# Attention products of the second block from split operands, in a two-block layer kernel

## The chip, the core and the metric

The kernel runs on one core of a Trainium2 chip. The metric is the device time of one execution in microseconds. A core has five engines that run their own instruction streams and meet only at semaphores: TensorE (PE in the profile; its weight loads are PEld), VectorE (DVE), ScalarE (ACT), GpSimd (POOL) and SyncE (SP), which here only issues loads.

## What is computed

Two layers in sequence on 512 tokens of width 2048, in fp32. Each is a wide input projection, several mixers, an output projection, a scaled residual and a layer norm. Block 0 mixes with forgetting attention, a short convolution and pooling. Block 1, on which the change works, has attention over selected keys and a state-space mixer:

```
u = einsum('bsd,de->bse', h, w_in)
q, k = rope(q), rope(k)                    # 8 query heads, 2 key/value heads, 128 wide
score = sum over 16 index heads of relu(q_idx . k_idx) * w_idx
_, sel = lax.top_k(score, 128)             # keys each query may attend to
s = (q . k[sel]) * scale ;  p = softmax(s) ;  o_attn = p . v[sel]
o = concat(o_attn * silu(z_attn), ssd(...))
h = layer_norm(alpha * h + o @ w_out)
```

The kernel does not gather. It finds the threshold by 16 rounds of eight maxima and masks all other keys. A block of 128 queries sees only keys up to its own end, so the score products have 128, 256, 384 and 512 columns.

## The kernel before

**Projections.** The weights stream through four slots, one unit of 128 x 1024 each, two units to a tile of 128 output features. For each unit SyncE loads `raw`, ScalarE rounds it to `w_hi` (`round_unit`, L870) and GpSimd computes `w_lo = raw - w_hi` (`low_part`, L409). TensorE multiplies in the one-pass format fp32r: `project` (L480) issues three matmuls of 512 columns for each of 16 row blocks, hi*hi, hi*lo and lo*hi, 48 for a tile. A unit keeps TensorE for about 5.5 us. ScalarE rounds a unit once the one four before it in the same slot has been used, so each unit has some 15 us from use to next use.

**Two kinds of small product.** `mm` on fp32 tiles is a true fp32 product; the trace shows it as two weight loads and two matmul records. `three` (L553) makes one product of three fp32r matmuls from high and low parts. In block 0 the scores and P.V of 256 columns and more already go through `three` (`attn_start1`, L558; `attn_pv1`, L567); the products of 128 columns are fp32 there. In block 1 all are fp32 (`head_scores`, `head_pv`).

**The heads of block 1.** TensorE's order is written out by hand. For head h of 1 to 7: the scores of attention head h-1 (`attn_start2`), the projection of the next q tile, the transposes of the probabilities (`head_turn`), the projection of the next gate tile, P.V (`head_pv`). Head 7's scores stand after the loop, and its transposes and P.V lie inside the output projection (`project_back`). The softmax runs meanwhile: VectorE adds the mask and finds the extremum (`head_softmax`), ScalarE takes exponentials (`head_exps`), VectorE scales (`head_scale`), copies the transposed probabilities from the banks to SBUF (`head_take_turned`), rotates the next q (`rope_head`), and after P.V multiplies by the gate (`head_finish`). ScalarE's order in a head (`head_tiles2`) is: exponentials, two weight units, the copy of q, two more units, the gate. Each engine works strictly in its written order.

**Ahead of the first head.** VectorE runs the 16 rounds of the key search on `bias` (`V.max` and `V.match_replace`, three each per round), with the rotation of the first q ahead of round 13. ScalarE copies V from two banks to `vN`. GpSimd finishes the rotation of K (`rope_k`). TensorE projects the q and gate tiles of head 0 and then waits for `k_roped` and `v_ready`.

**The last head.** `cut_early` on ScalarE and `cut_back` on VectorE split the first four finished features (`planes_hi`, `planes_lo`) for the output projection. TensorE enters `project_back` only when the last gate has been copied (`acc_taken`).

Of the kernel before, what the change touches and what calls it, by code (L numbers as in the profile page):

```python
# [115 lines left out]
def block_kernel(nc, x_t, x_rows, w_fg, stream, params, pool_w, ln1, ln2, rope_idx, rope_qk, out):  # L116
# [7 lines left out]
    with ExitStack() as ctx:  # L124
        def sb(name, shape, dt=fp32):
            return ctx.enter_context(nc.sbuf_tensor(name, shape, dt))
# [18 lines left out]
        qT = sb("qT", [P, S])  # L145
        vT = sb("vT", [P, S])
        gT = sb("gT", [P, S])
# [6 lines left out]
        probsT = sb("probsT", [P, QB, S])  # L154
        wide = sb("wide", [P, D])
# [36 lines left out]
        pT_hi = nc.alloc_sbuf_tensor_at("pT_hi", [P, 3, S], fp32r, offset=probsT_at)  # L192

# [85 lines left out]
        qk_hi, qk_ready, v_high, pT_high = sem("qk_hi"), sem("qk_ready"), sem("v_high"), sem("pT_high")  # L279
        v_turned, v_ready = sem("v_turned"), sem("v_ready")  # L280
# [173 lines left out]
        def _(pe):  # L454
# [70 lines left out]
            def head_scores(g):  # L525
                for i in range(QB):
                    n = P * (i + 1)
                    mm(B[i][:, 0:n], qT[:, P * i:n], kT[:, g, 0:n]).then_inc(scores_done, 1)

# [7 lines left out]
            def head_pv(a, g, dst=O):  # L537
                pe.wait_ge(probsT_ready, a + 1)
                for j in range(QB):
                    last = mm(dst[:, P * j:S], vN[:, g, j, :], probsT[:, j, P * j:S], j == 0, j == QB - 1)  # L540
                last.then_inc(pv_done, 1)
# [289 lines left out]
            pe.wait_ge(k_roped, 2)  # L831
            pe.wait_ge(v_ready, HEADS + 2)

            def attn_start2(g, h_ready):
                pe.wait_ge(q_roped, h_ready)
                head_scores(g)
# [17 lines left out]
        def _(act):  # L854
# [411 lines left out]
            take(t, tmp[:, :], T_HEAD2 - SK + 1)  # L1266
            for g, src in ((0, O), (1, M)):
                act.wait_ge(v_turned, HEADS + 1 + g)
                signal(nc.scalar.activation(vN[:, g, :, :].rearrange("p j n -> p (j n)"), src[:, :], ACT.Copy),
                       v_ready, HEADS + 1 + g)  # L1270
# [4 lines left out]
            def head_tiles2(h):  # L1275
                head_exps(HEADS + h - 1)
                load_table(ACT.Silu)
                t = tile_at(T_HEAD2, 0, h, 2)
                turn_round(t)
                act.wait_ge(q_roped, h)  # L1280
                take(t, tmp[:, :], T_HEAD2 - SK + 2 * h + 1)
                t = tile_at(T_HEAD2, 1, h, 2)
                if isinstance(h, int):
                    round_unit(t[0] + 1, 2 * t[1])
                    cut_early(1, T_BACK2)
                    round_unit(t[0] + 1, 2 * t[1] + 1)
                else:
                    turn_round(t)
                act.wait_ge(feat_done, 16 + 2 * GROUPS + h)
                take_gate(t, T_HEAD2 - SK + 2 * h + 2)  # L1290
                load_table(ACT.Exp)
# [4 lines left out]
            back_and_norm(1, T_BACK2, h_rows, {EARLY + 1: lambda: head_exps(2 * HEADS - 1)})  # L1296
# [3 lines left out]
        def _(dve):  # L1300
# [48 lines left out]
            def head_take_turned(a):  # L1349
                dve.wait_ge(probs_turned, a + 1)  # L1350
                for j in range(QB):
                    ins = V.tensor_copy(probsT[:, j, P * j:S], B[j][:, P * j:S])
                    if j < QB - 1:
                        step(ins)
                    else:
                        signal(ins, probsT_ready, a + 1)

# [18 lines left out]
            def low_probs(a):  # L1376
                dve.wait_ge(probs_turned, a + 1)
                step(V.tensor_copy(probsT[:, QB - 1, S - P:S], B[QB - 1][:, S - P:S]))  # L1378
                for j in range(QB - 1):
                    cols = slice(P * j, S)  # L1380
                    dve.wait_ge(pT_high, 3 * a + j + 1)
                    ins = V.tensor_sub(pT_lo[:, j, cols], B[j][:, cols], pT_hi[:, j, cols].bitcast(fp32))
                    if j < QB - 2:
                        step(ins)
                    else:
                        signal(ins, probsT_ready, a + 1)
# [418 lines left out]

            def rope_head(h):
                dve.wait_ge(acc_taken, T_HEAD2 - SK + 2 * h + 1)
                rope(qT, tmp, P, rope_q, swap16, q_roped, h + 1, padded[:, 16:16 + S])

            for r in range(TOPK // 8):  # L1810
# [3 lines left out]
                if r == 13:  # L1814
                    dve.wait_ge(rope_q_loaded, 16)
                    rope_head(0)
                for i in range(1, QB):
                    n = P * (i + 1)
                    if r:
                        dve.wait_ge(keys_taken, 3 * (r - 1) + i)  # L1820
                    V.max(top8[:, i, :], bias[:, i, 0:n]).then_inc(keys_found, 1)
# [11 lines left out]
            def head2(h):  # L1833
                a = HEADS + h - 1
                head_softmax(a)
                head_scale(a)
                head_take_turned(a)
                rope_head(h)

# [13 lines left out]
            head_take_turned(a)  # L1853
# [105 lines left out]
```

## Time and profile before

| | |
|---|---|
| time, median of 3 runs | 1727.95 us (1725.14 to 1729.54) |
| profiled execution | 1727.94 us, its span 1726.2 us |
| TensorE busy | 1710.0 us, 99% |
| VectorE, ScalarE, GpSimd busy | 723.7 us (42%), 615.8 us (36%), 697.6 us (40%) |
| chain that ended last | TensorE 94%, VectorE 3% |
| DMA | 186.16 MB, mean 108 GB/s |

The span is divided on the page into 40 slices, and TensorE is busy in nine tenths or more of each but the last. Matmul records overlap, because each contains the time until its end leaves the array: two matmuls of 512 columns that start 0.23 us apart are each listed with 0.39 us. Costs on TensorE are therefore best read from start to start. The profile names a wait after the instruction that released it.

### The profile page before, as it was taken

To read this page: it belongs to the slowest core of one execution; us is meant where nothing else is said; L and a number is where in the kernel's file an instruction comes from. 1 tells how busy PE (TensorE), PEld (TensorE's weight loads), DVE (VectorE), ACT (ScalarE), POOL (GpSimd) and SP (SyncE) were. 2 spreads that over 40 slices of the span, in tenths; PEclk is the share of its full clock that TensorE was granted. 3 is DMA by queue.
4 is the path that set the end of the run, shared out by engine and by line. 5 is a ranking of instruction groups with operands and counts; after the bars stand their busy time and mean duration, and the time that the engine had idled before them with its cause. 6 is when DMAs were issued, how large, how long until landed. Compare 5 with 4: busy or idle time off the path is not lost.

```text
span 1726.2 us, 21738 instructions
## 1 busy us (share of the span) xinstructions
PE 1710.0 (99%) x7958; PEld 1399.2 (81%) x7958; DVE 723.7 (42%) x1246; ACT 615.8 (36%) x851; POOL 697.6 (40%) x301
## 2 busy tenths in 40 slices
PE   9999999999999999999999999999999999999997
PEld 8888888888888888888888888887668787788886
DVE  4323321222111135211752744738679634465226
ACT  6434433443222224212642323423452434362120
POOL 4433343333444444445244434334226333325451
PEclk9999999999999999999999999999999999999999
DMA  6433323323233332543154342434123222227332
GB/s 225 121 92 92 90 87 92 99 88 94 92 98 97 98 90 94 170 122 106 65 197 129 116 132 88 134 103 118 49 76 98 84 75 73 83 61 269 121 97 98
DMA packets 56222, 186.16 MB, mean 108 GB/s; under 512 B 5928, under 2 KB 6184, under 8 KB 55376
## 3 DMA queue, kind: packets, MB, share of 16 engines
q1 hardware_dynamic: 46512, 160.19, 30.2%
q10 hardware_dynamic: 9632, 24.88, 4.1%
q8 instruction: 55, 0.90, 0.2%
q14 instruction: 23, 0.19, 0.0%
HBM read 176.57 MB, written 8.47 MB: 107 GB/s over the span
## 4 chain that ended last, share of the span: by engine, by line
PE 94%; DVE 3%; issue 1%; ACT 1%; POOL 0%; DMA 0%; SPq 0%; DVEq 0%; ACTq 0%; POOLq 0%
PE bank L456 92%; PE bank L460 2%; POOL w_lo L409 0%; DVE feats L1309 0%; DVE padded L1587 0%; DMA probsT<-decay_dram 0%; ACT w_hi L870 0%; DVE probs L1588 0%; DVE probs L1589 0%; DVE padded L1586 0%; DVE planes_lo L1529 0%; DVE kT L1688 0%; DVE wide L1697 0%; DVE bank L1522 0%; DVE tmp L1413 0%
## 5 line engine op out<-in xcount | busy, mean ns | idle before, releaser
L409 POOL TENSOR_TENSOR w_lo<-raw,w_hi 128x1024 fp32r<-128x1024 f32 x272 | 663.0, 2439 | 987.3 <-ACT w_hi L870 987.2
L456 PE MATMUL bank<-planes_hi,w_hi 128*128 128x512 f32 (+1 forms) x1792 | 705.8, 394 | 0.9 <-DVE planes_lo L1529 0.4
L456 PE MATMUL bank<-planes_lo,w_hi 128*128 128x512 f32 (+1 forms) x1792 | 691.8, 386 | 0.0
L456 PE MATMUL bank<-planes_hi,w_lo 128*128 128x512 f32 (+1 forms) x1776 | 686.4, 387 | 0.0
L870 ACT ACTIVATE w_hi<-raw 128x1024 fp32r<-128x1024 f32 x276 | 292.7, 1060 | 940.8 <-PE bank L456 909.3
L456 PEld LDWEIGHTS bank<-planes_hi,w_hi 128*128 128x128 f32 x1792 | 337.0, 188 | 84.1 <-issue 17.1
L456 PEld LDWEIGHTS bank<-planes_lo,w_hi 128*128 128x128 f32 x1792 | 337.3, 188 | 68.6 <-issue 3.3
L456 PEld LDWEIGHTS bank<-planes_hi,w_lo 128*128 128x128 f32 x1776 | 334.0, 188 | 67.8
L456 PE MATMUL bank<-w_hi,planes_hi 128*128 128x512 f32 x480 | 188.1, 392 | 0.0
L456 PE MATMUL bank<-w_hi,planes_lo 128*128 128x512 f32 x480 | 187.0, 390 | 0.0
L456 PE MATMUL bank<-w_lo,planes_hi 128*128 128x512 f32 x480 | 186.9, 389 | 0.0
L456 PEld LDWEIGHTS bank<-w_hi,planes_hi 128*128 128x128 f32 x480 | 90.2, 188 | 18.9 <-issue 0.2
L456 PEld LDWEIGHTS bank<-w_lo,planes_hi 128*128 128x128 f32 x480 | 90.1, 188 | 18.9 <-issue 0.5
L456 PEld LDWEIGHTS bank<-w_hi,planes_lo 128*128 128x128 f32 x480 | 90.1, 188 | 18.9
L1361 DVE TENSOR_TENSOR feats<-bank,gate 128x512 f32 (+1 forms) x16 | 11.1, 692 | 120.9 <-PE bank L456 120.9
L1378 DVE COPY probsT<-bank 128x128 f32<-128x128 f32 x8 | 2.3, 291 | 140.8 <-PE bank L460 140.8
L1443 DVE TENSOR_TENSOR padded<-kT,vT 128x512 f32<-128x512 f32 x4 | 9.2, 2301 | 117.6 <-ACT gate L895 117.6
L1309 DVE SCALAR_TENSOR_TENSOR feats<-probs,bank 128x512 f32<-128x512 f32 x16 | 11.0, 688 | 94.4 <-PE bank L456 94.2
L1320 DVE TENSOR_TENSOR planes_lo<-feats,planes_hi 128x512 fp32r<-128x512 f32 x48 | 43.1, 898 | 16.3 <-ACT planes_hi L916 14.8
L1309 DVE SCALAR_TENSOR_TENSOR feats<-bias,bank 128x512 f32<-128x512 f32 x16 | 11.0, 687 | 89.6 <-PE bank L456 89.2
L902 ACT ACT_TABLE_LOAD x35 | 44.9, 1283 | 1.1 <-ACT vT L895 0.5
L908 ACT ACTIVATE probs<-probs,nmax 128x128 f32<-128x128 f32 (+1 forms) x64 | 36.1, 564 | 12.1 <-DVE nmax L1339 7.9
(283 smaller groups left out, 1329.9 us busy)
## 6 DMA issues: line engine op xcount, KB each, us to landing
raw<-in_stream SPq DMA_DIRECT2D x281, 512.0 KB, 3.6
h_rows<-feats ACTq DMA_DIRECT2D x4, 1024.0 KB, 9.1
feats<-in_x_t SPq DMA_DIRECT2D x7, 512.0 KB, 9.3
out<-feats ACTq DMA_DIRECT2D x7, 512.0 KB, 2.7
rope_q<-cum_dram ACTq DMA_DIRECT2D x8, 256.0 KB, 3.0
bias<-in_x_rows ACTq DMA_DIRECT2D x2, 1024.0 KB, 6.1
probs<-in_x_rows ACTq DMA_DIRECT2D x2, 1024.0 KB, 7.9
rope_q<-decay_dram SPq DMA_DIRECT2D x8, 256.0 KB, 5.4
```

Of the source, the lines that this page charges most:

```text
L409: nc.gpsimd.tensor_sub(w_lo[:, s, :], raw[:, s, :], w_hi[:, s, :].bitcast(fp32)).then_inc(lo_ready, 1)
L456: return nc.tensor.matmul(o, a, b, start=start, stop=stop)
L460: return nc.tensor.transpose(o, a, ident[0:k, 0:k])
L870: signal(nc.scalar.activation(w_hi[:, s, :], raw[:, s, :], ACT.Copy), hi_ready, 4 * m + s - 3 if value is None else value)
L902: step(nc.scalar.activation(table_of[:, :], ones[:, 0:1], func))
L908: signal(nc.scalar.activation(probs[:, i, 0:n], probs[:, i, 0:n], ACT.Exp, bias=nmax[:, i:i + 1], scale=-1.0, accum_out=rowsum[:, i:i + 1] ...
L1309: return V.scalar_tensor_tensor(out=o, in0=a, scalar=scalar, in1=b, op0=op0, op1=op1)
L1320: signal(V.tensor_sub(planes_lo[:, k, :], feats[:, k, :], planes_hi[:, k, :].bitcast(fp32)), planes_ready, value)
L1361: signal(V.tensor_mul(feats[:, at(tile), :].rearrange("p a n -> p (a n)"), src[:, :], gate[:, :]), feat_done, count)
L1378: step(V.tensor_copy(probsT[:, QB - 1, S - P:S], B[QB - 1][:, S - P:S]))
L1443: step(V.tensor_mul(padded[:, 16:16 + S], kT[:, 0, :], vT[:, :]))
```

## The change

In block 1, scores and P.V of 256 columns and more are made of three fp32r matmuls from high and low parts; products of 128 columns stay fp32. New work follows from it:

- V: ScalarE rounds three of the four 128-column blocks of each of the two V tiles from their banks (`v2_hi`), VectorE subtracts (`v2_lo`) and copies the fourth (`low_v2`). Before, ScalarE copied all four.
- K: ScalarE rounds (`k2_hi`) and VectorE subtracts (`k2_lo`), 512 columns for each of two K tiles (`low_k2`).
- q of each head: ScalarE rounds columns 128 to 511 (`round_q2`), VectorE subtracts (`low_q2`).
- P transposed, each head: `round_probs` on ScalarE makes `pT_hi`, `low_probs` on VectorE makes the low parts, in the place of `head_take_turned`.

The V, K and first q steps of VectorE stand ahead of round 15 of the key search. TensorE additionally waits for `k2_ready` ahead of the first scores and for `q2_ready` in every head between the first and the second score product. ScalarE rounds q between the two units of a gate tile. The new tiles lie over memory that is free at that time.

```diff
-            def head_scores(g):
-                for i in range(QB):
-                    n = P * (i + 1)
-                    mm(B[i][:, 0:n], qT[:, P * i:n], kT[:, g, 0:n]).then_inc(scores_done, 1)
...
             def head_pv(a, g, dst=O):
                 pe.wait_ge(probsT_ready, a + 1)
-                for j in range(QB):
-                    last = mm(dst[:, P * j:S], vN[:, g, j, :], probsT[:, j, P * j:S], j == 0, j == QB - 1)
-                last.then_inc(pv_done, 1)
+                for j in range(QB - 1):
+                    cols = slice(P * j, S)
+                    three(dst[:, cols], v2_hi[g][:, j, :], v2_lo[g][:, j, :], pT_hi[:, j, cols], pT2_lo[j][:, :], j == 0, False)
+                mm(dst[:, S - P:S], vN[:, g, QB - 1, :], probsT[:, QB - 1, S - P:S], False, True).then_inc(pv_done, 1)
...
             pe.wait_ge(k_roped, 2)
+            pe.wait_ge(k2_ready, 2)
             pe.wait_ge(v_ready, HEADS + 2)
 
             def attn_start2(g, h_ready):
                 pe.wait_ge(q_roped, h_ready)
-                head_scores(g)
+                mm(B[0][:, 0:P], qT[:, 0:P], kT[:, g, 0:P]).then_inc(scores_done, 1)
+                pe.wait_ge(q2_ready, h_ready)
+                for i in range(1, QB):
+                    n, rows = P * (i + 1), slice(P * (i - 1), P * i)
+                    three(B[i][:, 0:n], q2_hi[:, rows], q2_lo[:, rows], k2_hi[g][:, 0:n], k2_lo[g][:, 0:n], True, True)\
+                        .then_inc(scores_done, 1)
...
+            def round_q2(h):
+                act.wait_ge(q_roped, h + 1)
+                signal(nc.scalar.activation(q2_hi[:, :], qT[:, P:S], ACT.Copy), q2_high, h + 1)
+
             for g, src in ((0, O), (1, M)):
                 act.wait_ge(v_turned, HEADS + 1 + g)
-                signal(nc.scalar.activation(vN[:, g, :, :].rearrange("p j n -> p (j n)"), src[:, :], ACT.Copy),
-                       v_ready, HEADS + 1 + g)
+                signal(nc.scalar.activation(v2_hi[g][:, :, :].rearrange("p j n -> p (j n)"), src[:, 0:3 * P], ACT.Copy),
+                       v_high, HEADS + 1 + g)
+            act.wait_ge(k_roped, 2)
+            for g in range(2):
+                signal(nc.scalar.activation(k2_hi[g][:, :], kT[:, g, :], ACT.Copy), k2_high, g + 1)
+            round_q2(0)
...
                 take(t, tmp[:, :], T_HEAD2 - SK + 2 * h + 1)
+                round_probs(HEADS + h - 1)
                 t = tile_at(T_HEAD2, 1, h, 2)
+                round_unit(t[0] + 1, 2 * t[1])
+                round_q2(h)
                 if isinstance(h, int):
-                    round_unit(t[0] + 1, 2 * t[1])
                     cut_early(1, T_BACK2)
-                    round_unit(t[0] + 1, 2 * t[1] + 1)
-                else:
-                    turn_round(t)
+                round_unit(t[0] + 1, 2 * t[1] + 1)
...
-            back_and_norm(1, T_BACK2, h_rows, {EARLY + 1: lambda: head_exps(2 * HEADS - 1)})
+            back_and_norm(1, T_BACK2, h_rows, {EARLY + 1: lambda: head_exps(2 * HEADS - 1), EARLY + 3: lambda: round_probs(2 * HEADS - 1)})
...
+            def low_v2():
+                for g, src in ((0, O), (1, M)):
+                    dve.wait_ge(v_high, HEADS + 1 + g)
+                    step(V.tensor_sub(v2_lo[g][:, :, :].rearrange("p j n -> p (j n)"), src[:, 0:3 * P],
+                                      v2_hi[g][:, :, :].rearrange("p j n -> p (j n)").bitcast(fp32)))
+                    signal(V.tensor_copy(vN[:, g, QB - 1, :], src[:, 3 * P:S]), v_ready, HEADS + 1 + g)
+
+            def low_k2():
+                for g in range(2):
+                    dve.wait_ge(k2_high, g + 1)
+                    signal(V.tensor_sub(k2_lo[g][:, :], kT[:, g, :], k2_hi[g][:, :].bitcast(fp32)), k2_ready, g + 1)
+
+            def low_q2(h):
+                dve.wait_ge(q2_high, h + 1)
+                signal(V.tensor_sub(q2_lo[:, :], qT[:, P:S], q2_hi[:, :].bitcast(fp32)), q2_ready, h + 1)
...
                     rope_head(0)
+                if r == 15:
+                    low_v2()
+                    low_k2()
+                    low_q2(0)
...
                 head_scale(a)
-                head_take_turned(a)
+                low_probs(a, low2)
                 rope_head(h)
+                low_q2(h)
```

## Rows read from the trace of the kernel before

**Rows 1.** The page, part 1: busy time and share of the span.
```profile
PE 1710.0 (99%) x7958; PEld 1399.2 (81%) x7958; DVE 723.7 (42%) x1246; ACT 615.8 (36%) x851; POOL 697.6 (40%) x301
```
**Rows 2.** TensorE's waits, whole span: total, times, longest (us); the longest first.
```profile
PE bank L456 <- ACT bias L1225: 3.0, 1, 3.0
```
**Rows 3.** Timeline of TensorE at a block 1 boundary: start, us, operation, count.
```profile
1396.71 2.32 PE L456 MATMUL bank<-probsT,vN 128*128 128x512 f32 x8
...
1401.26 0.40 PE L456 MATMUL bank<-planes_lo,w_hi 128*128 128x512 f32 x1
...
1423.98 2.32 PE L456 MATMUL bank<-probsT,vN 128*128 128x512 f32 x8
```
**Rows 4.** Timeline of TensorE in block 0: scores, then P.V.
```profile
108.53 0.38 PE L456 MATMUL bank<-kT,qT 128*128 128x128 f32 x2
108.66 0.36 PE L456 MATMUL bank<-k_hi,q_hi 128*128 128x256 f32 x1
...
110.32 0.39 PE L456 MATMUL bank<-planes_hi,w_hi 128*128 128x512 f32 x1
...
144.11 0.40 PE L456 MATMUL bank<-pT_hi,v_hi 128*128 128x512 f32 x1
...
146.14 0.39 PE L456 MATMUL bank<-planes_lo,w_hi 128*128 128x512 f32 x1
```
**Rows 5.** Timeline of TensorE at the first head of block 1.
```profile
1344.32 2.32 PE L456 MATMUL bank<-kT,qT 128*128 128x128 f32 x8
...
1346.72 0.40 PE L456 MATMUL bank<-planes_lo,w_hi 128*128 128x512 f32 x1
...
1357.41 1.25 PE L460 MATMUL bank<-ident,probs 128*128 128x128 f32 x10
```
**Rows 6.** Timeline of VectorE: first rope, round 15, last scaled row.
```profile
1334.63 0.01 DVE L1586 LOAD_MASK_SELECT padded<-tmp  x1 [3.28 <-issue]
...
1344.31 1.47 DVE L1821 MAX8 top<-bias 128x8 f32<-128x256 f32 x3
...
1356.24 0.49 DVE L1346 TENSOR_SCALAR probs<-probs,rinv 128x512 f32<-128x512 f32 x1
```
**Rows 7.** Block 0's splitting: by tile (ns min/median/max), and by line (busy us, mean ns).
```profile
L1367 DVE TENSOR_TENSOR v_lo<-bank,v_hi x8: 557/558/558, 55.8 to 397.2; 128x384 fp32r<-128x384 f32 x8
L1374 DVE TENSOR_TENSOR k_lo<-kT,k_hi x8: 692/693/2766, 44.4 to 382.1; 128x512 fp32r<-128x512 f32 x8
L1369 DVE COPY vN<-bank 128x128 f32<-128x128 f32 x8 | 2.3, 292 | 0.3
```
**Rows 8.** Timeline of GpSimd while VectorE is in round 15.
```profile
1345.71 2.39 POOL L409 TENSOR_TENSOR w_lo<-raw,w_hi 128x1024 fp32r<-128x1024 f32 x1 [3.02 <-ACT w_hi L870]
```
**Rows 9.** Timelines of GpSimd, VectorE and ScalarE in the last head.
```profile
1529.31 2.41 POOL L409 TENSOR_TENSOR w_lo<-raw,w_hi 128x1024 fp32r<-128x1024 f32 x1 [4.47 <-ACT w_hi L870]
1534.46 2.36 POOL L409 TENSOR_TENSOR w_lo<-raw,w_hi 128x1024 fp32r<-128x1024 f32 x1 [2.73 <-ACT w_hi L870]
...
1530.01 4.45 DVE L1320 TENSOR_TENSOR planes_lo<-feats,planes_hi 128x512 fp32r<-128x512 f32 x4 [2.40 <-ACT planes_hi L916]
1535.49 0.69 DVE L1361 TENSOR_TENSOR feats<-bank,gate 128x512 f32<-128x512 f32 x1 [1.03 <-PE bank L456]
...
1536.26 0.60 ACT L895 ACTIVATE gate<-bank 128x512 f32<-128x512 f32 x1 [1.88 <-DVE feats L1361]
```
**Rows 10.** TensorE in windows (length, busy, granted clock, DMA), and its first timeline row.
```profile
1715.00:1716.00 1.00, 0.02 (x1) 1.00 0.00 0
1719.00:1720.00 1.00, 0.00 (x0) 0.98 1.01 401
...
1.13 5.93 PE L456 MATMUL bank<-probs 128*128 128x128 f32 x28 [1.13 <-DVE probs L1394]
```
**Rows 11.** Timelines of VectorE and ScalarE in the head that ends at rows 3's next boundary.
```profile
1417.83 0.69 DVE L1589 TENSOR_TENSOR qT<-qT,padded 128x512 f32<-128x512 f32 x1
...
1418.83 1.06 ACT L870 ACTIVATE w_hi<-raw 128x1024 fp32r<-128x1024 f32 x1 [4.89 <-PE bank L456]
```

More of the change, by code:

```diff
@@ L145, in block_kernel @@
         qT = sb("qT", [P, S])
+        vT_at = nc.sbuf_base
         vT = sb("vT", [P, S])
+        gT_at = nc.sbuf_base
         gT = sb("gT", [P, S])
@@ L154, in block_kernel @@
         probsT = sb("probsT", [P, QB, S])
+        wide_at = nc.sbuf_base
         wide = sb("wide", [P, D])
@@ L192, in block_kernel @@
         pT_hi = nc.alloc_sbuf_tensor_at("pT_hi", [P, 3, S], fp32r, offset=probsT_at)
+        pT2_lo = [nc.alloc_sbuf_tensor_at(f"pT2_lo{j}", [P, S - P * j], fp32r, offset=wide_at + 4 * a)
+                  for j, a in enumerate((0, S, 2 * S - P))]
+        v2_lo = [nc.alloc_sbuf_tensor_at(f"v2_lo{g}", [P, 3, P], fp32r, offset=wide_at + 4 * (9 + 3 * g) * P) for g in range(2)]
+        v2_hi = [nc.alloc_sbuf_tensor_at(f"v2_hi{g}", [P, 3, P], fp32r, offset=vN_at + 4 * S * g) for g in range(2)]
+        k2_hi = [nc.alloc_sbuf_tensor_at(f"k2_hi{g}", [P, S], fp32r, offset=a)
+                 for g, a in enumerate((feats_at + 4 * 4 * S, vT_at))]
+        k2_lo = [nc.alloc_sbuf_tensor_at(f"k2_lo{g}", [P, S], fp32r, offset=feats_at + a * 4 * S) for g, a in enumerate((5, 7))]
+        q2_hi = nc.alloc_sbuf_tensor_at("q2_hi", [P, S - P], fp32r, offset=gT_at)
+        q2_lo = nc.alloc_sbuf_tensor_at("q2_lo", [P, S - P], fp32r, offset=probsT_at + 3 * 4 * S)
         causal = rope_q[:, 1, :]
@@ L279, in block_kernel @@
         qk_hi, qk_ready, v_high, pT_high = sem("qk_hi"), sem("qk_ready"), sem("v_high"), sem("pT_high")
+        k2_high, k2_ready, q2_high, q2_ready = sem("k2_high"), sem("k2_ready"), sem("q2_high"), sem("q2_ready")
         v_turned, v_ready = sem("v_turned"), sem("v_ready")
@@ L1347, in head_scale @@
                            probs_scaled, 4 * a + i + 1)
[L1349 to L1356, printed above, removed]
             def head_finish(a, tile, count, gate_taken, src=O):
@@ L1374, in low_qk, with low_probs @@
                     signal(V.tensor_sub(lo[:, :], src, hi[:, :].bitcast(fp32)), qk_ready, 2 * h + j + 1)
-            def low_probs(a):
+            def low_probs(a, low=lambda j: pT_lo[:, j, P * j:S]):
                 dve.wait_ge(probs_turned, a + 1)
@@ L1381, in low_probs @@
                     dve.wait_ge(pT_high, 3 * a + j + 1)
-                    ins = V.tensor_sub(pT_lo[:, j, cols], B[j][:, cols], pT_hi[:, j, cols].bitcast(fp32))
+                    ins = V.tensor_sub(low(j), B[j][:, cols], pT_hi[:, j, cols].bitcast(fp32))
                     if j < QB - 2:
@@ L1804, in shuffle_k, with low2 @@
                 signal(V.stream_shuffle((vT, gT)[g][:, :], kT[:, g, :], swap16), k_shuffled, g + 1)
+            def low_v2():
[11 more added lines that the diff above has]
+                signal(V.tensor_sub(q2_lo[:, :], qT[:, P:S], q2_hi[:, :].bitcast(fp32)), q2_ready, h + 1)
+            def low2(j):
+                return pT2_lo[j][:, :]
             def rope_head(h):
@@ L1852, in _ @@
             cut_back(1, 7, 8)
-            head_take_turned(a)
+            low_probs(a, low2)
             cut_back(1, 8, 9)
```

## The prediction

> **What bounds the kernel now.** I read the page's part 1 first: TensorE is busy 99% of the span [rows 1]. Its list of waits comes next, because a busy share counts pipelined matmuls as longer than they are: the longest single wait in 1726 us is 3.0 us, and there is no wait at all among the heads of block 1 [rows 2]. So there TensorE's own instructions set the time. Whatever shortens them is worth its full size, and whatever makes TensorE wait costs its full size. The other engines matter only where they come later than TensorE does. After that I read the timelines of four places: one ordinary boundary between heads, its counterpart in block 0 (which already uses the three-product form), the first head of block 1 and the last.
>
> **What the cheaper products save.** At an ordinary boundary TensorE runs P.V of one head and then the scores of the next. In block 1 these start at 1396.71; the second projection matmul after them starts at 1401.26, and projection matmuls stand 0.23 apart, so the pair takes 1401.03 - 1396.71 = 4.32 us [rows 3]. (I take the second one because the first overlaps the end of the last fp32 product.) In block 0 the scores take 110.32 - 108.53 = 1.79 us and P.V takes 146.14 - 0.23 - 144.11 = 1.80 us [rows 4], together 3.59. The shapes and the one fp32 product of 128 columns in each are those of the changed block 1. A pair saves 0.73 us, and there are seven: 5.1 us. The first scores stand alone, 1346.72 - 0.23 - 1344.32 = 2.17 us before [rows 5] and 1.79 after: 0.38. The last P.V stands alone too and gives half a pair, 0.36. Sum: 5.85 us. The Trainium skill ("FP8 and Floating Point Precision", TensorE Precision Notes) says that true fp32 takes four passes. Three in place of four, on the 1152 of 1280 columns that change, would save a quarter of 4.32 x 0.9, 0.97 us a pair, and some 7.8 us in all (an estimate by that page); the rows of block 0 contain what surrounds the passes, and I go by them.
>
> **What the new preparation costs at the first head.** VectorE now makes the low parts of V (two subtractions of 384 columns, two copies of 128), of K (two of 512) and of the first q (one of 384), all placed ahead of round 15 of the top-key search. TensorE waits for V and K before the first scores, and for q before their second product. Before the change, round 15 starts at 1344.31 [rows 6] and the first scores start at 1344.32 [rows 5]. The work is put exactly where TensorE arrives, so nothing hides it. Step by step: V costs 2 x (0.56 + 0.29) [rows 7] and some 0.04 after each, to 1346.17. K's subtraction reads two SBUF tiles. GpSimd starts such a subtraction at 1345.71 and holds it until 1348.10 [rows 8]; ScalarE and GpSimd get there as before, since they follow TensorE's last projection. What VectorE does meanwhile is shown in two places: the same kind of subtraction took 0.692 at the least and 2.766 at the most in block 0 [rows 7], and four of them took 4.45 in the last head, where three are worth 0.73 each and the first therefore 2.26, from 1530.01 to 1532.27, which is 0.56 after GpSimd's end (1529.31 + 2.41 = 1531.72) [rows 9]. So K0 ends at 1348.10 + 0.56 = 1348.66, K1 at 1349.39, and q at 1349.98. The three split products and what follows are worth 110.32 - 108.66 = 1.66 us [rows 4], so the projection starts at 1351.7 and not at 1346.49: 5.2 us later, in which the 0.38 gained is already contained. The stall by itself is 5.6 us. Bounds: 4.2 if GpSimd does not hold VectorE (K at 0.73 each), 7 if it holds it twice.
>
> Behind VectorE's added work stand round 15 and the first softmax. From the start of round 15 to the last scaled row were 1356.73 - 1344.31 = 12.42 us [rows 6], so now 1350.0 + 12.4 = 1362.4. TensorE's transposes moved from 1357.41 [rows 5] to about 1362.6, and they need the last row 0.6 later. That delay is covered, but with well under 1 us to spare. ScalarE's copies of V and K come while it is idle, and the q copy after rope ends ahead of its next weight unit: nothing.
>
> **The clock.** TensorE would stand still for some 5.0 us. The trace grants full clock through the 3.0 us wait [rows 2]. At the end of the kernel, the last matmul ended just after 1715.0 and the clock went to half (2.4 to 1.2 GHz) at about 1719.98, some 5.0 us later [rows 10]. So this gap lies just where the clock can fall. What that costs is shown at the start: 28 records of 128 columns took 5.93 us, 0.21 each, against (1.25 - 0.27) / 9 = 0.11 each for the ten transposes of the same width [rows 5]: about 3.0 us lost [rows 10]. (The clock column does not show that stretch as slow, so I use it as an upper bound only.) Bounds 0 and 3.0; I take 1.0, because the gap is about as long as the shortest one that shows a fall. The Trainium skill ("TensorE: Matmul & The Clock Gate", The HAM clock gate) says that an idle array falls to half rate and needs sustained work to come back; by it every run in which the fall happens pays the re-warming, and the sum would be 1730.7 instead of 1728.7.
>
> **The ordinary heads.** ScalarE now rounds P transposed (three copies, of 0.60 at most, which is what 512 columns from a bank took [rows 9]) and VectorE subtracts instead of copying: VectorE ends about 1.0 later than before. The rotated q, ready at 1418.52 before (1417.83 + 0.69), is ready at 1419.5. ScalarE has its unit until 1419.89, rounds q until 1420.4, and VectorE subtracts 0.56, or waits for one whole GpSimd operation of 2.4: q ready by 1421 to 1423 [rows 11]. TensorE asks for it after P.V, at about 1423.98 + 1.8 + 0.2 = 1426.0 [rows 3]. Cover: 3 us or more; P.V has over 7. Queued behind ScalarE's wait for q is one weight unit, which TensorE needs some 10 us later. Cost: nothing.
>
> **The last head.** VectorE gets the q subtraction ahead of four subtractions for the output projection, and behind those stands the multiplication by the gate, for which ScalarE's next gate and then TensorE wait. Before, the four ended at 1534.46, the multiplication started at 1535.49 and the gate copy at 1536.26 [rows 9]. Now q goes in at about 1529.9, is held until 1531.72 and ends near 1532.15; the four end near 1535.1, and P.V, shorter by 0.37, allows the multiplication at 1535.12. The gate is ready near 1536.5 and TensorE arrives at 1536.65 (in before's time): no cost. But the fourth subtraction starts at 1534.36, and GpSimd starts at 1534.46 [rows 9]. In the output projection ScalarE rounds P before it goes on with its cuts. From the transposes' end that is up to 1.8 for P, seven cuts at some 0.65, 1.06 for a unit [rows 11] and 2.4 on GpSimd [rows 8], under 10.5 us; TensorE has two units (48 matmuls at 0.23) and P.V before it, 12.7 us. Covered by some 2 us.
>
> **The sum.** -5.85 + 5.6 + 1.0 = +0.75 on the profiled execution's 1727.94 us, whose median neighbour is 1727.95: 1728.7 us.
>
> **Rivals.** (1) The gain is kept: the preparation is hidden, the clock holds, and the time is 1727.94 - 5.85 = 1722.1. For it: VectorE has idle time earlier (it waits 3.28 us ahead of the first rope [rows 6]). Against it: the work is queued ahead of round 15, behind that idle time. If only GpSimd's hold is missing, it is 1727.94 - 5.85 + 4.2 = 1726.3. (2) Slower: in the last head GpSimd wins the race for the fourth subtraction. It decides if VectorE is 0.1 us later than worked out. The subtraction then ends at 1534.46 + 2.36 + 0.56 = 1537.38, multiplication and gate end near 1538.8, and TensorE waits 2.2 us: 1730.9. The skill ("SBUF — State Buffer", Who interferes with whom) says that whoever starts first holds the port for the whole instruction; by it VectorE wins at the times above and the sum stays; no row shows two starts so close. (3) The clock falls and costs its full 3.0: 1730.7; with (2) 1732.9.
>
> **How the numbers follow.** Forecast 0.55; gain kept whole 0.06; no hold at the first head 0.09; (2) 0.15; (3) 0.12; both 0.03. The range takes in the missing hold below and the single slower cases above, with half a microsecond and the spread of the runs: 1725.8 to 1731.8. Within 0.3% (5.2 us; about what a measurement of this kernel can tell from no change) lie all cases but the gain kept whole, which misses it by little on the other side, and the double one if anything is added to it. Faster 0.07, same 0.85, slower 0.08.
>
> **What would show it.** In the profile after: a wait of TensorE of about 5 us near 1344.4, for VectorE's low part of K; a K subtraction of over 2 us beside GpSimd; heads that repeat every 26.54 us and not every 1423.98 - 1396.71 = 27.27 [rows 3]; the granted clock after the gap; and the gate of the last head. The forecast is wrong if TensorE does not wait there, if a pair saves other than 0.73, or if a wait for q appears in every head.

## The result, and the profile after

The changed kernel takes 1730.31 us in the median (1728.28 to 1732.25, 20 runs) where the kernel before takes 1728.13 (1725.14 to 1729.61, 20 runs): ratio 1.0013, 95% interval 1.0007 to 1.0019. The profiled execution took 1732.25 us, its span 1730.1. The forecast was 1728.7 (+0.75), with a difference within 0.3% as the likeliest outcome (0.85). The median rose by 2.18 us, 0.13%: the interval lies clear of 1, and the difference well within 0.3%. The account below is that the mechanism was right, that the term for the clock was too small, and that 0.34 us outside the span was missing.

The page's part 1 of the changed kernel, to be read against [rows 1], and its list of waits of TensorE (total, times, longest), against [rows 2]:

```profile
PE 1707.6 (99%) x8006; PEld 1404.8 (81%) x8006; DVE 746.5 (43%) x1260; ACT 633.2 (37%) x885; POOL 700.3 (40%) x301
```

```profile
PE bank L470 <- DVE k_lo L1831: 5.2, 1, 5.2
PE bank L470 <- ACT bias L1241: 3.0, 1, 3.0
PE bank L470 <- DVE planes_lo L1344: 1.2, 1, 1.2
```

Again 99% busy, and that says as little as it did before. The list of waits tells it: the old wait of 3.0 us is there, and a new one of 5.2 us, for the low part of K. The one of 1.2 us is new too, but lies at 6.4 us, at the very start of the kernel, where the change touches nothing (experiment 6). No head waits for its q. Where the new wait lies is in TensorE's timeline (start, duration, operation, idle time before it in brackets), the counterpart of [rows 5]:

```profile
1345.92 0.39 PE L470 MATMUL bank<-planes_hi,w_lo 128*128 128x512 f32 x1
1351.46 0.79 PE L470 MATMUL bank<-kT,qT 128*128 128x128 f32 x2 [5.16 <-DVE k_lo L1831]
...
1354.93 0.63 PE L470 MATMUL bank<-planes_hi,w_hi 128*128 128x512 f32 x1
1355.36 0.63 PE L470 MATMUL bank<-planes_lo,w_hi 128*128 128x512 f32 x1
...
1356.93 0.40 PE L470 MATMUL bank<-planes_hi,w_lo 128*128 128x512 f32 x1
1357.16 0.39 PE L470 MATMUL bank<-planes_hi,w_hi 128*128 128x512 f32 x1
...
1366.69 0.49 PE L474 MATMUL bank<-ident,probs 128*128 128x128 f32 x3
```

TensorE is ready for the scores at 1345.92 + 0.23 = 1346.15 and gets them at 1351.46: 5.31 us. Then the matmuls themselves are slow: the scores take 1354.93 - 1351.46 = 3.47 us, not 1.79, and the first projection matmuls stand 0.43 apart, not 0.23. TensorE in windows of 1 us (length, busy, records, granted clock, DMA) says why:

```profile
1348.00:1349.00 1.00, 0.00 (x0) 1.00 0.00 0
1349.00:1350.00 1.00, 0.00 (x0) 0.96 0.00 0
1350.00:1351.00 1.00, 0.00 (x0) 0.50 0.00 0
1351.00:1352.00 1.00, 0.54 (x3) 0.50 1.03 188
...
1355.00:1356.00 1.00, 1.00 (x4) 0.50 0.00 0
1356.00:1357.00 1.00, 1.00 (x4) 0.62 0.00 0
1357.00:1358.00 1.00, 1.00 (x6) 1.00 0.00 0
```

The granted clock fell from 2.4 to 1.2 GHz at about 1349.9, when TensorE had stood still for 3.8 us, and came back at about 1356.8, when it had been at work again for over 5 us. (A slice's mean gives the moment: 0.62 between 1356 and 1357 is half clock until 1356.76.) What keeps K waiting is on VectorE and GpSimd (timelines of the two, to be read against [rows 6] and [rows 8]):

```profile
1346.13 0.55 DVE L1824 TENSOR_TENSOR v_lo<-bank,v_hi 128x384 fp32r<-128x384 f32 x1
...
1347.96 3.18 DVE L1831 TENSOR_TENSOR k_lo<-kT,k_hi 128x512 fp32r<-128x512 f32 x2
1351.17 0.56 DVE L1835 TENSOR_TENSOR q_lo<-qT,q_hi 128x384 fp32r<-128x384 f32 x1
```

```profile
1347.53 2.34 POOL L423 TENSOR_TENSOR w_lo<-raw,w_hi 128x1024 fp32r<-128x1024 f32 x1 [3.02 <-ACT w_hi L886]
```

VectorE begins the V steps at the very moment TensorE arrives (1346.13 and 1346.15), and K's two subtractions take 3.18 us together, one of them 0.69: the first lasts 2.45 us, until 0.55 us after GpSimd's end at 1349.87.

**The balance in four numbers.** Everything is cut at three points of TensorE: its arrival at block 1's first scores (A), the start of head 0's transposes (T, the row 1366.69 above, 1357.41 in [rows 5]) and the start of the last matmul of the kernel (E). The last matmuls of both kernels:

```profile
1714.63 0.39 PE L456 MATMUL bank<-w_hi,planes_lo 128*128 128x512 f32 x1
```

```profile
1718.54 0.39 PE L470 MATMUL bank<-w_hi,planes_lo 128*128 128x512 f32 x1
```

| us | A | A to T | T to E | A to E |
|---|---|---|---|---|
| before | 1344.32 | 13.09 | 357.22 | 370.31 |
| after | 1346.15 | 20.54 | 351.85 | 372.39 |

From T on the change gives back 5.37, and up to T it costs 7.45: together +2.08. The two profiled executions lie 4.31 apart. Of the rest, 1.83 came before A, where the change touches nothing, and 0.4 lies outside the span (1732.25 - 1730.1 = 2.15 against 1.74). Both are taken up below.

### The profile page after: what moved, and what is told of

It is laid out like the page before. It is cut to its first block, busy times and chain, and to the rows that moved or that the text cites. A ratio compares the mean times of both kernels' runs of the same rounds, so it can differ in the third digit from the quotient of the medians.

```text
span 1730.1 us, 21953 instructions
## 1 busy us (share of the span) xinstructions
PE 1707.6 (99%) x8006; PEld 1404.8 (81%) x8006; DVE 746.5 (43%) x1260; ACT 633.2 (37%) x885; POOL 700.3 (40%) x301
## 4 chain that ended last, share of the span: by engine, by line
PE 93%; DVE 4%; issue 2%; ACT 1%; DMA 1%; POOL 0%; ACTq 0%; DVEq 0%; SPq 0%; POOLq 0%
PE bank L470 91%; PE bank L474 2%; DVE padded L1602 0%; POOL w_lo L423 0%; DVE feats L1333 0%; DMA probsT<-decay_dram 0%; ACT w_hi L886 0%; DVE probs L1603 0%; DVE probs L1604 0%; DMA feats<-in_x_t 0%; DVE bias L1863 0%; DVE padded L1601 0%; DVE k_lo L1831 0%; DVE top L1859 0%; DVE planes_lo L1544 0%
```

## The experiments

All runs stand beside runs of the kernel before on the same chip. There are three groups, each on a chip of its own. In the first (k_first, filler, hidden) the kernel before took 1728.31 us, in the second (prep_only2, hidden_scores, hidden_late, hidden_warm) 1727.81, in the third (before_warm, after_warm, filler_warm, warm_late) 1728.18 (medians of 22, 21 and 33 runs). Where medians of two groups are compared, half a microsecond between them means little; the traces are then set beside them.

**1. The order of the preparation: k_first.** The theory: K's hold by GpSimd is a matter of when it comes.

```diff
-                    low_v2()
                     low_k2()
+                    low_v2()
                     low_q2(0)
```

> VectorE's new work ahead of round 15 in another order: K first, then V, then q. Nothing else differs from the changed kernel. Theory (GpSimd's subtraction holds VectorE's subtractions of two SBUF tiles): K now starts 1.4 us ahead of GpSimd's operation and each K subtraction takes 0.69 us, not 3.18 for both; TensorE's wait at the first head falls from 5.2 to about 3.4 us and the kernel gains 1.8 us, 1728.5, and another 2 us if the clock then holds. Rival (K's subtraction is slow because both its inputs are in SBUF, whoever else runs): both still take over 3 us and the time stays at 1730.3.

Measured: 1728.97 us (1727.92 to 1729.58, 11 runs), ratio 1.0003 [0.9994, 1.0012]. VectorE and TensorE in its timelines:

```profile
1344.28 1.41 DVE L1831 TENSOR_TENSOR k_lo<-kT,k_hi 128x512 fp32r<-128x512 f32 x2
1345.72 0.56 DVE L1824 TENSOR_TENSOR v_lo<-bank,v_hi 128x384 fp32r<-128x384 f32 x1
...
1347.55 0.88 DVE L1835 TENSOR_TENSOR q_lo<-qT,q_hi 128x384 fp32r<-128x384 f32 x1
```

```profile
1347.89 0.79 PE L470 MATMUL bank<-kT,qT 128*128 128x128 f32 x2 [3.45 <-DVE vN L1826]
```

K's two subtractions now take 1.41 us and end just as GpSimd starts (1345.67, until 1348.01); V's, one of whose sources is a bank, take 0.56 beside GpSimd as without it, and q's, of two SBUF tiles again, takes 0.88 and not 0.56. So the hold falls on subtractions of two SBUF tiles. The wait went down by 1.7 us, but not the fall of the clock: it came at about 1346.5, only 2.2 us after A (1344.29), and the low stretch again lasted until 1353.3. A to E is 370.83, 0.52 over the kernel before. The median lies 1.3 us under that of the changed kernel, where 1.8 was expected; so the first theory holds, and the better case, in which the clock stays up, did not come.

**2. The clock by itself: filler.** TensorE waits as long as before but is given work whose result nobody reads.

```diff
             pe.wait_ge(k_roped, 2)
+            for e in range(20):
+                mm(B[3][:, :], planes_hi[:, e % KT, 0:P], planes_hi[:, e % KT, :])
             pe.wait_ge(k2_ready, 2)
```

> The changed kernel with 20 filler matmuls of 512 columns, into a bank whose contents are then overwritten, ahead of TensorE's wait at the first head. They take about 4.5 of its 5.3 us and move no other step. Theory (some 2 us of the change's time are the fallen clock): granted clock stays at full level, the score products at the first head take 0.11 to 0.23 us each as elsewhere, and the time falls by 2.2 us to 1728.1. Rival (the clock cost nothing at the end, the stall alone does it): the time stays at 1730.3.

Measured: 1728.99 us (1726.74 to 1730.18, 11 runs), ratio 1.0004 [0.9995, 1.0013]. TensorE's timeline:

```profile
1344.22 4.69 PE L470 MATMUL bank<-planes_hi 128*128 128x512 f32 x20
1349.51 0.48 PE L470 MATMUL bank<-kT,qT 128*128 128x128 f32 x2 [0.59 <-DVE k_lo L1833]
```

The scores come 5.29 us after A, as in the changed kernel, and at this head every window is at full clock. A to T is 18.31 us, so the changed kernel's 20.54 holds 2.23 us of half pace. The medians show 1.3 (2.2 was expected), but each carries the scatter of the pause at 1207 us (experiment 6), which is as large.

**3. Preparation without products: prep_only2.** All roundings, subtractions, buffers and waits of the change, with the products as they were:

```diff
-                    cols = slice(P * j, S)
-                    three(dst[:, cols], v2_hi[g][:, j, :], v2_lo[g][:, j, :], pT_hi[:, j, cols], pT2_lo[j][:, :], j == 0, False)
+                    mm(dst[:, P * j:S], v2_hi[g][:, j, :].bitcast(fp32), pT_hi[:, j, P * j:S].bitcast(fp32), j == 0, False)
...
-                    three(B[i][:, 0:n], q2_hi[:, rows], q2_lo[:, rows], k2_hi[g][:, 0:n], k2_lo[g][:, 0:n], True, True)\
-                        .then_inc(scores_done, 1)
+                    mm(B[i][:, 0:n], qT[:, P * i:n], kT[:, g, 0:n]).then_inc(scores_done, 1)
```

> Everything that the change adds in preparation and waits stays (the rounding of k and v of block 1, the subtractions, the differences of the probabilities, the buffers and their waits); the products are matmuls of fp32 as in the kernel before. The P.V products read the high parts of the probabilities and of v alone and the scores the high parts of q and k; the low parts' share of the result is left out. My theory: the three-product form gains by the matmuls alone, so this kernel loses what the change loses and gains nothing: 1728.3 + 5.3 (wait at block 1's first scores) + about 2.2 (half-pace stretch behind it) = about 1735.8 us, ratio 1.0043, and the heads of block 1 come every 27.27 us as in the kernel before, not every 26.53. Rival, the one that would take the loss away from the preparation: a good part of the gain of 0.74 us a head comes from reading rounded operands or from the order of the heads, and then the period is under 27.0 and the time near 1730 to 1732.

(The scores read q and k unsplit, as the diff shows, and not the high parts. P.V reads the high parts alone; the low parts' share of the result is left out.) Measured: 1736.14 us (1735.64 to 1738.06, 5 runs), ratio 1.0051 [1.0037, 1.0064]. The transposes of two heads:

```profile
1365.47 1.25 PE L474 MATMUL bank<-ident,probs 128*128 128x128 f32 x10
1392.75 1.25 PE L474 MATMUL bank<-ident,probs 128*128 128x128 f32 x10
```

The period is 27.28 us, and T to E is 357.22, that of the kernel before to the hundredth. The added steps cost nothing in any head, the last included; the whole gain is in the matmuls, the whole loss in front of T.

**4. The preparation where VectorE and GpSimd are idle: hidden.** K is rounded and subtracted ahead of the first rotation of q; the low parts of V and of the first q go to GpSimd between its weight units; TensorE asks for V only before the first P.V. GpSimd subtracts from copies of V in SBUF that ScalarE makes first. In outline:

```diff
+            low_part(m0 + 1, 0)
+            low_part(m0 + 1, 1)
+            pool.wait_ge(q2_high, 1)
+            nc.gpsimd.tensor_sub(q2_lo[:, :], qT[:, P:S], q2_hi[:, :].bitcast(fp32)).then_inc(q2_ready, 1)
+            low_part(m0 + 1, 2)
...
                 if r == 13:
                     dve.wait_ge(rope_q_loaded, 16)
+                    low_k2()
                     rope_head(0)
-                if r == 15:
-                    low_v2()
-                    low_k2()
-                    low_q2(0)
```

> The changed products with the preparation where the engines idle: K is rounded ahead of the second weight unit and subtracted on VectorE ahead of the first rope, where it waits 3.3 us; V's low parts and the first q's are made by GpSimd in its gaps, from copies that ScalarE makes; TensorE waits for V only ahead of the first P.V. Theory: no wait at the first head, the clock holds, heads repeat every 26.5 us, and the time is 1728.1 - 5.85 = 1722.3. Rival (work of that size costs its time wherever it stands): 1727 or more.

Measured: 1722.88 us (1720.94 to 1724.18, 6 runs), ratio 0.9965 [0.9953, 0.9977], 0.6 us over what was expected. The first scores and the projection behind them:

```profile
1345.60 0.39 PE L480 MATMUL bank<-planes_hi,w_lo 128*128 128x512 f32 x1
1345.83 0.38 PE L480 MATMUL bank<-kT,qT 128*128 128x128 f32 x2
...
1347.63 0.40 PE L480 MATMUL bank<-planes_hi,w_hi 128*128 128x512 f32 x1
```

No wait, no fall of the clock, the scores in 1.80 us. A to E is 1710.39 - 1345.83 = 364.56 us, 5.75 under the kernel before: what the cheaper products are worth by themselves (the forecast had 5.85).

**5. Which products pay: hidden_scores.** The kernel hidden with P.V as in experiment 3's first edit; as there, the low parts' share of P.V is left out.

> The kernel hidden, with the P.V products back as matmuls of fp32 (of the high parts of the probabilities and v alone; the low parts' share of the result is left out) and only the scores in three products. My theory: the scores' matmuls and the P.V matmuls of a head each hold half of the gain of 0.72 us, so the eight heads give back 8 x 0.36 = 2.9 us: 1722.9 + 2.9 = about 1725.8 us, the period of the heads 26.9 us. Rival: one of the two kinds holds nearly all of it (a matmul of fp32 of 128 columns after another format pays a switch that the other does not); then the time is either about 1723 (period 26.55) or about 1728.5 (period 27.27).

Measured: 1724.99 us (1722.26 to 1726.72, 11 runs), ratio 0.9985 [0.9976, 0.9994]. T to E is 1712.17 - 1357.73 = 354.44 us, against 351.84 in hidden and 357.22 before. So the eight P.V that lie behind T hold 2.60 us, 0.33 each, and the seven scores 2.78, 0.40 each. Both kinds pay; neither holds nearly all. The period of the heads is 26.87 us, as expected; the median came out 0.8 us lower than expected.

**6. The pause at 1207 us: hidden_warm, before_warm, after_warm, filler_warm.** Where did the 1.83 us ahead of A come from? TensorE's windows there, first of the kernel before, then of the changed one:

```profile
1208.00:1209.00 1.00, 0.00 (x0) 1.00 0.00 0
1209.00:1210.00 1.00, 0.00 (x0) 1.00 0.00 0
1210.00:1211.00 1.00, 0.91 (x4) 1.00 0.00 0
1211.00:1212.00 1.00, 1.00 (x4) 0.69 0.00 0
1212.00:1213.00 1.00, 1.00 (x4) 0.50 0.00 0
1213.00:1214.00 1.00, 1.00 (x5) 0.50 0.00 0
1214.00:1215.00 1.00, 1.00 (x5) 0.61 0.00 0
```

```profile
1209.00:1210.00 1.00, 0.00 (x0) 0.99 0.00 0
1210.00:1211.00 1.00, 0.34 (x2) 0.50 0.00 0
...
1215.00:1216.00 1.00, 1.00 (x4) 0.50 0.00 0
1216.00:1217.00 1.00, 1.00 (x5) 0.60 0.00 0
```

The 3.0 us wait for ScalarE [rows 2] lets the clock fall in both, but in the kernel before it fell at 1211.4, when TensorE had been at work again for 1.3 us, and stayed low for 3.4 us; in the changed one it fell at 1210.0 and stayed low until 1216.8. TensorE worked through 3.4 us of that in the one and 6.1 in the other (it resumed at 1210.66); half of the difference, 1.4 us, is the larger part of the 1.83 ahead of A. Another 0.56 was there before the pause began (1207.07 and 1207.63 in the two timelines); the changed kernel's profile has a wait of 1.17 us for first operands at 6.4 us that the other has not, and after_warm, with the same change, has none either. With the pause filled the two kernels reach A at the same time: 1342.88 us in before_warm, 1342.86 in after_warm. Four kernels fill it:

```diff
             def idx_scores(t, i):
                 pe.wait_ge(idx_roped, t + 1)
+                if t == 0 and i == 3:
+                    for e in range(12):
+                        mm(M[:, :], planes_hi[:, e, 0:P], planes_hi[:, e, :])
```

> The kernel hidden, with 12 matmuls on data at hand, whose result nobody reads, in the 3.0 us in which TensorE waits for ScalarE's bias rows in block 0 at about 1207 us. My theory: the pause is what lets the granted clock fall just behind it, for 3.3 to 6.7 us in every profile so far; with the pause filled the clock stays at its full level there, and the stretch of half pace, worth 1.6 to 3.3 us, goes: 1722.9 - 2.3 = about 1720.6 us (1719.6 to 1721.3), granted clock of the run 0.998 or more. Rival: the clock falls there for another reason (or the fillers delay the matmuls by as much as they save): 1722.9 us or a little more, the fall still at about 1211.

> The kernel before, with 12 matmuls that nobody reads in the 3.0 us pause of TensorE at 1207 us, as in hidden_warm; block 1 is untouched. My theory: the half-pace stretch behind that pause is there in the kernel before as well, has nothing to do with the change, and its varying length makes most of the spread of the runs. So this kernel is about 2.3 us faster than the one before, 1725.6 us (1725.0 to 1726.3), and its runs lie within 1 us of each other, where those of the kernel before span 3 us. Rival: the gain of hidden_warm over hidden (1722.9 to 1720.7) came from another place or from the chip; then 1727.8 us and a spread of 3 us.

> The changed kernel, with the same 12 matmuls at 1207 us. With the spread of that pause taken out on both sides, after_warm minus before_warm is the value of the change without noise. My theory, from the traces (wait 5.3, half-pace stretch behind it 2.3, products 7 x 0.74 and a little more at the end = 5.6 to 5.9): +1.7 to +2.3 us, so about 1727.7 us, granted clock 0.996. Rival: the 2.2 us between the medians of the changed kernel and the one before were in part the pause at 1207 (it cost 3.3 us in the changed kernel's profile and 1.7 in the other's); then the difference is only about 0.5 us, 1726.2 us.

> The kernel after_warm with the 20 matmuls of the kernel filler as well, which nobody reads, in the wait for K at block 1's first scores: the wait stays, the granted clock does not fall. My theory: the half-pace stretch is worth 2.2 us (the difference between the traces from the last projection matmul to the transposes, 20.54 against 18.31), so 1727.7 - 2.2 = about 1725.5 us, level with before_warm. Rival: only the 1.3 us by which filler's median lay under the changed kernel's, so 1726.4 us.

| kernel | median us (lowest to highest, runs) | ratio to before |
|---|---|---|
| hidden_warm | 1720.68 (1720.40 to 1721.03, 5) | 0.9960 [0.9946, 0.9973] |
| before_warm | 1726.49 (1725.96 to 1726.99, 11) | 0.9992 [0.9983, 1.0001] |
| after_warm | 1728.39 (1727.76 to 1729.09, 11) | 1.0001 [0.9992, 1.0010] |
| filler_warm | 1726.66 (1726.43 to 1726.97, 11) | 0.9991 [0.9982, 1.0000] |

Windows of hidden_warm over the same stretch:

```profile
1209.00:1210.00 1.00, 0.97 (x5) 1.00 0.00 0
1210.00:1211.00 1.00, 0.82 (x4) 1.00 0.00 0
1211.00:1212.00 1.00, 1.00 (x5) 1.00 0.00 0
```

The clock stays up, and the scatter goes: the runs of each of the four lie within 0.5 to 1.3 us, while those of the kernel before span over 3. The 76 runs of the kernel before beside the experiments stand in three groups by their mean granted clock: 17 at 0.998 with a median of 1726.57 us, 45 at 0.997 with 1728.18, 14 at 0.996 with 1729.37. The group at 0.998 is level with before_warm. That the groups are no fall, a short one and a long one at 1207 us is inferred from these numbers; only single executions were profiled. It also says why before_warm gained 1.7 us and not the expected 2.3: the short case is the usual one in the kernel before.

With that scatter gone, the change costs 1728.39 - 1726.49 = 1.90 us (about 1.6 to 2.1 by resampling the runs), and the half pace at block 1's first head is worth 1728.39 - 1726.66 = 1.73, between the 2.2 of filler_warm's theory and the 1.3 of its rival; from A to T the two traces differ by 1.57. The products with hidden preparation give 1720.68 - 1726.49 = -5.81; these two are of different groups, but their traces say the same (A at 1342.88 in both, A to E 364.55 against 370.30: -5.75). The rival of after_warm, a difference of 0.5 us, is out.

**7. The race in the last head: hidden_late, warm_late.** Three reciprocals that nobody reads push VectorE's four subtractions 0.6 us later, in hidden and in hidden_warm:

```diff
             head2(HEADS - 1)
+            for _ in range(3):
+                step(V.reciprocal(rinv[:, 0:1], rowsum[:, 0:1]))
             cut_back(1, 0, EARLY)
```

> The kernel hidden, with three reciprocals of one column that nobody reads on VectorE ahead of the last head's four subtractions (about 0.2 us each), so that the fourth subtraction comes behind the start of GpSimd's 2.55 us operation and not ahead of it. This prices the prediction's second rival, the race in the last head. That rival's theory: VectorE's fourth subtraction is held until GpSimd's operation ends and the end of the kernel comes 2.1 us later: 1722.9 + 2.1 = about 1725.0 us. The other theory: the two engines do not hold each other there (the subtraction reads PSUM or is short), or TensorE has other work: at most the 0.6 us of the reciprocals, 1722.9 to 1723.5.

> The kernel hidden_warm with the three reciprocals of hidden_late: the price of the last head's race without the spread of the pause at 1207. My theory: the held subtraction delays TensorE by 2.0 us and the kernel by 2.3 (the two traces from the last head's P.V products to the last matmul: 180.6 and 182.9 us), so 1720.7 + 2.3 = about 1723.0 us in every run. Rival: in part of the runs the granted clock also falls behind that 2.0 us pause (the medians of hidden_late and hidden lay 3.4 us apart); then the runs stand in two groups, near 1723.0 and near 1724.5, the later ones with a lower clock.

The changed kernel won the race, as the forecast had it (timelines of VectorE and GpSimd, the counterpart of [rows 9]):

```profile
1536.73 2.87 DVE L1344 TENSOR_TENSOR planes_lo<-feats,planes_hi 128x512 fp32r<-128x512 f32 x4
```

```profile
1539.30 2.55 POOL L423 TENSOR_TENSOR w_lo<-raw,w_hi 128x1024 fp32r<-128x1024 f32 x1 [3.02 <-ACT w_hi L886]
```

The fourth subtraction starts at 1538.91, 0.4 us ahead of GpSimd (the forecast had 0.1). In hidden_late it starts behind it:

```profile
1527.31 0.56 DVE L1895 RECIPROCAL rinv<-rowsum 128x1 f32<-128x1 f32 x3
1527.90 4.94 DVE L1357 TENSOR_TENSOR planes_lo<-feats,planes_hi 128x512 fp32r<-128x512 f32 x4
```

```profile
1529.89 2.40 POOL L423 TENSOR_TENSOR w_lo<-raw,w_hi 128x1024 fp32r<-128x1024 f32 x1 [3.03 <-ACT w_hi L896]
```

```profile
1534.30 0.50 PE L480 MATMUL bank<-w_hi,planes_hi 128*128 128x512 f32 x1 [2.03 <-ACT gate L921]
```

The four end at 1532.84, again 0.55 after GpSimd's end, and TensorE waits 2.03 us for the gate. From the start of the last P.V but one to E it is 182.9 us, against 180.6 in hidden: 2.3 us, where the second rival had 2.2. The Trainium skill ("SBUF — State Buffer", Who interferes with whom) says that VectorE and GpSimd share a port, held as an exclusive lock, and that the order of issue decides who blocks. The traces agree: the fourth subtraction takes 0.69 us where it starts 0.4 us ahead of GpSimd (changed kernel) and 2.76 where it starts 0.2 us behind (hidden_late). In the changed kernel GpSimd's operation then takes 2.55 us, against a median of 2.40. The medians were 1726.31 us (1724.70 to 1726.80, 11 runs), ratio 0.9990 [0.9981, 0.9999], and for warm_late 1724.42 (1722.65 to 1725.27, 11 runs), ratio 0.9977 [0.9968, 0.9986]. They lie 3.4 us over hidden and 3.7 over hidden_warm (each of another group), where about 2.1 and 2.3 were expected; by the traces, A to E in warm_late is 366.89 us against hidden_warm's 364.55, 2.34 more. The runs of warm_late stand in two groups, as its rival had it, five from 1722.65 to 1723.41 and six from 1724.42 to 1725.27. The profiled one is of the first and shows full clock behind the wait. A fall of the clock behind a wait of 2.0 us in the second group would explain the 1.6 us between them, and their mean granted clock is a little lower; no profile shows it.

## Why the prediction was right, and which term was off

- **What bounds it** [rows 1, 2]: right. What TensorE's products saved and what TensorE waited came through one to one.
- **The products** [rows 3, 4, 5]: right, 5.75 against 5.85. A pair takes 1541.51 - 1537.91 = 3.60 us (P.V of the last head but one to the projection), forecast 3.59; the period of the heads is 1393.22 - 1366.69 = 26.53 us, forecast 26.54. The 7.8 us that a count of passes gives is not borne out.
- **The stall** [rows 5 to 8]: right. Filler shows it alone, 5.29 us until the scores and 0.3 until TensorE is in step again (18.31 - 12.72 = 5.59), forecast 5.6. The first K subtraction ended 0.55 us after GpSimd, as read from [rows 9] (0.56). The lower bound of 4.2 was added up wrongly: without the hold the prediction's own steps end K and q 1.76 us sooner, which leaves 5.6 - 1.76 = 3.8, and that case at 1725.9 us and not 1726.3. In k_first, where K is not held, the scores start 3.60 us after A.
- **The clock** [rows 10]: the mis-sized term. I took 1.0; it is 1.7 by the medians of the warm kernels, 1.6 by their traces and 2.2 in the changed kernel's profiled execution. What came is rival (3), a fall of the clock, to which I gave 0.12, at half to three quarters of its price of 3.0. The step that failed is the sentence that the trace grants full clock through the 3.0 us wait. It does, through the wait; 1.3 us behind it the clock was down, in the very trace I had, and I stopped reading where the wait ended. Read to the end, that place says that 3.0 us of idleness were enough there; for 5 us the fall was then the likely case, and the term no compromise between 0 and 3.0. It can be worked out: in each profile in which the clock fell at this place the low stretch lasted 6.8 us, and it costs about half of the time for which TensorE works within it.

| us | scores start | clock back | half of the time between | measured |
|---|---|---|---|---|
| after | 1351.46 | 1356.76 | 2.65 | 2.23 |
| k_first | 1347.89 | 1353.34 | 2.73 | 2.39 |
| prep_only2 | 1350.13 | 1354.52 | 2.20 | 1.93 |
| after_warm | 1348.14 | 1352.06 | 1.96 | 1.56 |

The last column is A to T over that of filler (18.31), corrected for the wait in k_first (5.29 - 3.60) and the dearer scores in prep_only2 (0.38). It follows the fourth at a distance of 0.3 to 0.4. The cost thus depends on how late in the low stretch TensorE resumes, and k_first, with the shorter wait, pays more for the clock (2.39 against 2.23). The Trainium skill ("TensorE: Matmul & The Clock Gate", The HAM clock gate) says that an idle array falls to half rate and needs sustained work to come back; all four traces agree. That 1730.7 lies near the measured 1730.3 is in part luck: it prices the re-warming at 3.0, where 1.6 to 2.4 was measured, and contains neither the 0.34 us below nor the pause at 1207 us.

- **The ordinary heads and the last one** [rows 9, 11]: right. No wait for q in any head; prep_only2 puts the price of all added steps behind T at 0.00.
- **Missing from the sum:** 0.34 us outside the span. Run time less span is 2.07 us in the changed kernel and in every kernel that keeps its preparation (mean of each, 2.06 to 2.11), and 1.73 in the kernel before and in all of the hidden ones. Its cause stays open.

The sum with the measured terms: -5.75 + 5.59 + 1.56 + 0.34 = +1.74 us for after_warm over before_warm, by their traces; their medians say 1.90. The forecast had +0.75. Rival (1), the gain kept whole, was a real option, but for another place of the work: hidden is that kernel. The range held because the errors were small beside its width of 6 us; nothing in it tells +0.75 from +1.9.

## What to carry to other kernels

A stall in front of TensorE has two prices, the idle time and the half-pace stretch behind it. Read the granted clock for several microseconds past the end of every pause, not only through it. When a product is made cheaper by splitting its operands, the splitting has to be put into idle time of VectorE and GpSimd before the first product that needs it: the same work at another place turned about +2 us into -5.4 (hidden, by the medians). And fill or remove a pause that every run has before comparing variants: here it took most of the scatter away, and 12 matmuls that nobody reads were worth 1.7 us in the unchanged kernel; with both, hidden_warm is 0.4% faster than the kernel before.

## What the runs showed of the hardware

- The clock fell 2.2 us (k_first), 3.8 us (after) and some 5 us (end of the kernel before, [rows 10]) after TensorE had run out of matmuls, so idle time alone doesn't fix the moment. Behind the 3.0 us pause it fell in all eight profiles that have the pause, in five of them 0.3 to 1.4 us after TensorE had resumed.
- Once it fell at block 1's first head, it was low for 6.8 us each time; at 1207 us for 3.4 us in some profiles and 6.8 in others.
- A VectorE subtraction of two SBUF tiles of 512 columns that meets a running GpSimd subtraction ended 0.55 us after it, one of 384 columns 0.41 us (k_first); one with a source in a bank took 0.56 us either way. In prep_only2, whose products are unchanged, the added steps behind T cost nothing (357.22 us from T to E in both): there they fell into idle time of their engines.
